# Three weight tiles ahead on ScalarE, one-hots of four tokens at once, and row fetches before bulk loads, in the gate stage of a two-layer kernel

## The reference

```python
vals, ci = lax.top_k(cand, P_TOPK)
e = (jnp.take_along_axis(i1, ci // P_TOPK, axis=-1) * N_KEYS
     + jnp.take_along_axis(i2, ci % P_TOPK, axis=-1))
g = jax.nn.softmax(vals, axis=-1)
...
a = jnp.einsum('cd,ckd->ck', xc, expert_u[ec])
w = (gc * jax.nn.gelu(a.astype(jnp.float32))).astype(x.dtype)
return jnp.einsum('ck,ckd->cd', w, expert_v[ec])
```

## Time and profile before

| what | value |
|---|---|
| median of 3 runs | 2543.64 us |
| profiled execution | 2543.99 us, its span 2542.3 us |
| busy share of the span | PE 94%, DVE 58%, ACT 44%, POOL 15% |
| chain that ended last | PE 77%, DVE 12%, ACT 8%, DMA 1%, issue 1% |
| GELU of the U jobs (L1397) | 128 x 491 ns |
| `whi` (L410) and `wlo` (L414) | 398 x 1056 ns and 398 x 1225 ns |
| copies to `stage` (L1478) | 96 x 1132 ns |
| HBM traffic | 407.12 MB read, 52.43 MB written |

### The profile page before, as it was taken

One profiled execution on the slowest core, in us unless ns is written; L12 is line 12 of the kernel. 1 busy time (PEld: TensorE's weight loads), 2 busy tenths in 40 slices (PEclk: granted clock), 3 DMA queues, 4 the chain that ended last, 5 costly groups with the idle time before them and its releaser, 6 DMA issues.

```text
span 2542.3 us, 39573 instructions
## 1 busy us (share of the span) xinstructions
PE 2397.2 (94%) x14819; PEld 2116.5 (83%) x14819; DVE 1463.5 (58%) x3355; ACT 1115.1 (44%) x1958; POOL 374.0 (15%) x338
## 2 busy tenths in 40 slices
PE   7999999999999888999999998888878999999999
PEld 4888788888785555779999998888877999999999
DVE  4444444333654485441899998777758773444443
ACT  4444343222442376343433448877853332332322
POOL 0000000000200000100001002222334313433330
PEclk9999999999998799998999999999998999999999
DMA  4223222322430000121556658887899988999992
GB/s 151 99 74 100 90 97 77 100 88 87 163 107 21 1 1 1 50 100 67 160 160 188 203 167 290 292 282 274 286 335 357 340 285 327 347 362 332 357 352 102
DMA packets 131823, 462.11 MB, mean 182 GB/s; under 512 B 13840, under 2 KB 32528, under 8 KB 129888
## 3 DMA queue, kind: packets, MB, share of 16 engines
q1 hardware_dynamic: 75744, 233.87, 26.9%
q0 software_dynamic: 51440, 196.90, 21.5%
q10 hardware_dynamic: 4496, 29.36, 3.0%
HBM read 407.12 MB, written 52.43 MB: 181 GB/s over the span
## 4 chain that ended last, share of the span: by engine, by line
PE 77%; DVE 12%; ACT 8%; DMA 1%; issue 1%; POOL 0%; ACTq 0%; SPq 0%; DVEq 0%; POOLq 0%
PE bank L427 13%; PE bank L428 13%; PE bank L429 13%; PE bank L1092 7%; PE bank L1093 7%; PE bank L1094 7%; DVE wlo L414 3%; PE bank L1105 2%; ACT stage L1478 2%; PE bank L442 2%; ACT hot L1464 1%; PE bank L1060 1%; PE bank L524 1%; ACT hot L1459 1%; ACT whi L410 1%; PE bank L707 1%
## 5 line engine op out<-in xcount | busy, mean ns | idle before, releaser
L414 DVE TENSOR_TENSOR wlo<-raw,whi 128x1024 fp32r<-128x1024 f32 x398 | 485.5, 1225 | 540.0 <-ACT whi L410 482.3
L427 PE MATMUL bank<-act_hi,whi 128*128 128x384 f32 (+1 forms) x1968 | 730.4, 371 | 31.9 <-DVE wlo L414 18.4
L428 PE MATMUL bank<-act_lo,whi 128*128 128x384 f32 (+1 forms) x1968 | 718.8, 365 | 0.0
L429 PE MATMUL bank<-act_hi,wlo 128*128 128x384 f32 (+1 forms) x1968 | 718.0, 365 | 0.0
L410 ACT ACTIVATE whi<-raw 128x1024 fp32r<-128x1024 f32 x398 | 418.3, 1056 | 288.2 <-PE bank L1094 175.2
L427 PEld LDWEIGHTS bank<-act_hi,whi 128*128 128x128 f32 x1968 | 375.8, 191 | 81.5 <-DVE wlo L414 21.0
L429 PEld LDWEIGHTS bank<-act_hi,wlo 128*128 128x128 f32 x1968 | 375.5, 191 | 38.1
L428 PEld LDWEIGHTS bank<-act_lo,whi 128*128 128x128 f32 x1968 | 376.0, 191 | 35.7 <-issue 0.5
L1092 PE MATMUL bank<-h_hi,whi 128*128 128x384 f32 x1024 | 350.2, 342 | 6.5 <-DVE h_lo L2196 6.5
L1093 PE MATMUL bank<-h_lo,whi 128*128 128x384 f32 x1024 | 348.0, 340 | 0.0
L1094 PE MATMUL bank<-h_hi,wlo 128*128 128x384 f32 x1024 | 345.8, 338 | 0.0
(11 more groups left out here) (354 smaller groups left out, 2765.5 us busy)
## 6 DMA issues: line engine op xcount, KB each, us to landing
raw<-tiles SPq DMA_DIRECT2D x398, 512.0 KB
acts_dram<-gelu SPq DMA_DIRECT2D x128, 192.0 KB
gates_dram<-stage ACTq DMA_DIRECT2D x12, 2048.0 KB
wg<-gates_dram POOLq DMA_DIRECT2D x16, 1536.0 KB
hf<-acts_dram POOLq DMA_DIRECT2D x16, 1536.0 KB
bias<-alibi POOLq DMA_DIRECT2D x16, 256.0 KB, 3.0
w1s<-cmp_w POOLq DMA_DIRECT2D x1, 4096.0 KB, 13.8
res<-x_t ACTq DMA_DIRECT2D x4, 512.0 KB, 10.0
```

The lines of the kernel that those rows point to most:

```text
L414: dve.tensor_tensor(wlo[:, j.slot, :], raw[:, j.slot, :], whi[:, j.slot, :].bitcast(F32), ALU.subtract).then_inc(lo_made, 1)
L427: pe.matmul(to, wh, x, start=(kc == 0), stop=False)
L428: pe.matmul(to, wh, xl, start=False, stop=False)
L429: last = pe.matmul(to, wl, x, start=False, stop=(kc == KC - 1))
```

## The change

- ScalarE prepares `whi` three jobs ahead (HI_AHEAD) in the gate stage, in the U jobs behind it and in the V jobs. One extra `make_hi` ahead of the first step fills the gap. VectorE's `make_lo` stays at two.
- VectorE makes the four first one-hots of a group in one instruction (a comparison of two broadcast operands, 128 x 512), behind the two weighted ones.
- The copy to `stage` walks the same 512 elements in another order: before it read the bank densely and wrote every 32nd element; now it reads every 128th element of the bank and writes runs of 4 neighbours.
- 2 dots in every step (96 in the stage, before 80), then 1 in each of 8 jobs (before 2), then 24 in the V jobs (before 32). With them the steps that follow the last dot (V_HEAD, V_WEIGHTS, QUADS) come one group earlier.
- GpSimd issues loads for group 0, two row fetches, the loads for group 1, six row fetches and the memset, in that order.

```diff
-DOTS_GATES = [2, 2, 1]
-DOTS_REST = 2
+HI_AHEAD = 3
+DOTS_GATES = 2
+DOTS_REST = 1
-V_HEAD = 4
+V_HEAD = 3
-QUADS = {40 + r * 78 // 31: r for r in range(32)}
+QUADS = {32 + r * 86 // 31: r for r in range(32)}
...
             load_gates(0)
-            load_gates(1)
             for m in range(RING):
                 pool.wait_ge(acts_stored[m], 16 * 5)
             load_acts(0)
+            for n in range(SEEN_GATES + ROWS, SEEN_GATES + ROWS + 2):
+                gather(n)
+            load_gates(1)
             load_acts(1)
+            for n in range(SEEN_GATES + ROWS + 2, SEEN_U + ROWS):
+                gather(n)
             pool.memset(spread[0][:, :], 0.0).then_inc(S("spread_zeroed"), 1)
-            for n in range(SEEN_GATES + ROWS, SEEN_U + ROWS):
-                gather(n)
...
+            make_hi(act, Job(J_U + U_GATES).ahead())
             for q in range(DT // 8):
-                u_job(U_GATES + q)
+                u_job(U_GATES + q, HI_AHEAD)
...
-                    act.activation(stage[:, buf, :, t:t + 4].rearrange("p j t -> p t j"),
-                                   bank[4 + gi % 4][:, :].rearrange("p (t j) -> p t j", t=4),
+                    act.activation(stage[:, buf, :, t:t + 4],
+                                   bank[4 + gi % 4][:, :].rearrange("p (t j) -> p j t", t=4),
...
-                    for x in range(4):
-                        t = 4 * gi + x
-                        ins = dve.tensor_scalar(hot[:, gi % 4 * 4 + x, 0, :], iota, selT[:, 0, t:t + 1], None, ALU.is_equal)
-                        if x < 2:
-                            dve.tensor_scalar(hot[:, gi % 4 * 4 + x, 1, :], iota, selT[:, 1, t:t + 1],
-                                              selT[:, 2, t:t + 1], ALU.is_equal, ALU.mult)
-                    ins.then_inc(S("hot_made"), 1)
-                for _ in range(DOTS_GATES[q % 3]):
+                    t, slot = 4 * gi, gi % 4 * 4
+                    for x in range(2):
+                        dve.tensor_scalar(hot[:, slot + x, 1, :], iota, selT[:, 1, t + x:t + x + 1],
+                                          selT[:, 2, t + x:t + x + 1], ALU.is_equal, ALU.mult)
+                    dve.tensor_tensor(hot[:, slot:slot + 4, 0, :], iota.unsqueeze(1).broadcast_to((P, 4, P)),
+                                      selT[:, 0, t:t + 4].unsqueeze(2).broadcast_to((P, 4, P)),
+                                      ALU.is_equal).then_inc(S("hot_made"), 1)
+                for _ in range(DOTS_GATES):
```

More of the change, by code:

```diff
@@ L64 @@
 ROWS = 8
-DOTS_GATES = [2, 2, 1]
-DOTS_REST = 2
+HI_AHEAD = 3
+DOTS_GATES = 2
+DOTS_REST = 1
 DOTS_V = 1
-V_HEAD = 4
+V_HEAD = 3
 V_WEIGHTS = GJ * V_HEAD + 1
-QUADS = {40 + r * 78 // 31: r for r in range(32)}
-SEEN_GATES = sum(DOTS_GATES) * 16
+QUADS = {32 + r * 86 // 31: r for r in range(32)}
+SEEN_GATES = DOTS_GATES * DT // 8
 SEEN_U = SEEN_GATES + DOTS_REST * (P - U_REST)
@@ L1398, in activation_of, with u_job @@
                                ACT.Gelu_apprx_tanh).then_inc(taken[j.slot], 1)
-            def u_job(n):
+            def u_job(n, ahead=AHEAD):
                 j = Job(J_U + n)
-                make_hi(act, j.ahead())
+                make_hi(act, j.ahead(ahead))
                 activation_of(j, n // RING)
@@ L1485, in _ @@
             for n in range(U_REST, P):
-                u_job(n)
+                u_job(n, HI_AHEAD)
             def weigh_hi(grp, m):
@@ L1502, in _ @@
                     jj = GJ * grp + dc
-                    if not (last and dc + AHEAD >= KC):
-                        make_hi(act, Job(J_V + jj).ahead())
+                    if not (last and dc + HI_AHEAD >= KC):
+                        make_hi(act, Job(J_V + jj).ahead(HI_AHEAD))
                     if not last and dc >= LATE:
```

## The result

The changed kernel takes 2456.99 us (median of 4 runs, 2455.63 to 2459.88), the kernel before, beside it, 2546.16 us (4 runs, 2543.43 to 2550.14). The ratio is 0.965, 95% interval 0.9631 to 0.9669. The profiled execution has a span of 2454.1 us, 88.2 less than before, where 66.3 were forecast.

What follows compares the result with a forecast made beforehand. A circle of waits between engines was taken to bound the gate stage, late loads and a row fetch the passage behind it. From 2543.99 us, 45.6 (stage) and 20.7 (passage) came off: 2477.7, forecast 2478, range 2462 to 2508.

Steps and rivals of the forecast that it cites:

- The circle of waits: Gate stage: VectorE, ScalarE and TensorE wait for each other, 14.05 us per two jobs; three ahead makes it 4.7 a job.
- Rival 3: Gate stage: the circle is not the cause, another wait holds 7.37 us a step; 2523 us, chance 0.06.
- What is late next: Gate stage once the circle is open: ScalarE's 6.2 us plus 0.2 gives a 6.4 us step, gain 45.6 us.
- near equals: Gate stage: 0.2 us a step added because two or three engines of nearly equal work do not meet exactly.
- the passage: Last one-hot product to first V product: 57.7 us falls to 37, gain 20.7, bounds 8 and 23.
- ScalarE's own work: Gate stage: 6.02 us busy a step plus 0.2 for issuing gate stores, so 6.2.
- the signs that I named: Profile signs of being right, among them `whi` waits under 10 us, clock 1.00, ScalarE fullest, V product about 37 us behind.
- The copy: ScalarE's copy to `stage`: kept at 1132 ns, bounds 600 (ScalarE at 5.14 us a step) and 1490 ns (6.92).
- low end: Lower edge of the range: a gate-stage step of 6.1 us (gain 59.7) and 22 us behind the stage, 2462 us.
- One-hots and dots: VectorE, gate stage: joint comparison saves 0.4 us a step, extra dots cost 0.38; it stays at 5.75.
- Rival 1: Gate stage: DMA takes over, 6.7 us a step, a late gate store leaves 12 us behind; 2501 us, chance 0.16.
- Rivals 2 and 4: ScalarE's copy: at 1490 ns, 2502 us, chance 0.12; or strided PSUM read slows the kernel, 2569 us at 2.2 us, 0.05.

Runs made afterwards that it cites:

- the last experiment: Changed kernel without the third product (act_hi times wlo) in the 48 gate-stage jobs, leaving out part of the computation: 2447.88 us, one run.
- The early load: Changed kernel with group 0's activations loaded once TensorE has used the last one-hots, not behind the last gate store: 2456.47 us, in a second series 2452.39.

## Why the prediction was wrong

**The circle of waits** was read rightly. Three ahead opens it, and alone it takes the step from 7.37 to 5.97 us, 65.9 us of the stage. Rival 3 is out.

**What is late next** is the step that failed. I put ScalarE at 6.2 us and added 0.2 for near equals: 6.4. The step is 5.95, TensorE's own work. The stage gave 66.5 us where the sum had 45.6; these 20.9 us are the miss (88.2 - 66.3 = 21.9 in all; the passage is 0.3 under its term, and 1.3 lie ahead of the stage and behind the passage). Of the 0.45 us a step, 0.2 are ScalarE's own work, 0.2 the term for near equals, and the last 0.05 the lag that ScalarE could afford even with its old copy. Of the signs that I named, two did not come for this reason: the fullest engine is TensorE and not ScalarE, and the last one-hot product starts 281.5 us behind the first and not some 300.

- *ScalarE's own work* with the old copy is 6.00 us, not 6.2. I divided its busy time in a stage full of gaps by the steps, and then added the store issue. An instruction with a gap behind it counts in full, while back to back the next one starts before it ends: in the old-copy run a GELU of 0.46 us at 1701.59 is followed by the next instruction at 1701.96, and ScalarE is busy 254.94 us in 260, 5.85 a step, where the earlier trace rows gave 6.02. From GELU to the next GELU without a wait it is 5.83 us. In the trace before, one such turn was already 5.95 us (1702.79 to 1708.74). The store issue adds 0.17 a step, near the 0.2 that I allowed.
- *The copy* fell to the lower end of its bounds. I took the old 1132 ns, since one stride was traded for another; it is 579. ScalarE's own work is then 224.06 us busy in 260, 5.13 a step. But this did not matter for the step: with the old copy it is 5.96. The copy is worth some 5 us, 4.8 of them in the passage, where a late ScalarE delays the last store.
- *The 0.2 us for near equals* had no row behind them, and no run shows them. In the changed kernel with the old copy ScalarE (6.00), TensorE (5.95), VectorE (249.78 us busy in 260, 5.73) and a full DMA ran at 5.96 us a step. That the four slots of each buffer let one engine lag behind the others is my explanation; no run varied their number.

The bound of the stage was there in the earlier trace rows. My low end used 6.1 us for it and 22 us behind it, so the range ended at 2462, before the floor of 5.95 was reached. With that floor and my own term for the passage the sum is 2544 - 66.7 - 20.7 = 2456.6.

**One-hots and dots.** The price was right (683 ns), and nearly the saving: where VectorE sets the pace, a step is 6.04 us with single one-hots and 5.67 with the joint comparison (the last experiment), 0.37 less where I had 0.4. Single one-hots cost 0.09 us a step here, since VectorE passes TensorE by that much; I had counted the edit as free under a ScalarE at 6.2. The two edits belong together: the shorter one-hots pay for the extra dots.

**DMA.** The 362 GB/s of the earlier trace rows were not a limit. The Trainium skill (DMA: Bandwidth & Descriptors, Specifications) has 358 GB/s for a core that shares its HBM; 381 over 285 us, and 402 in the last experiment, stand against taking that as the bound here, where one core runs the program. Rival 1 is out.

**The read of PSUM.** Rivals 2 and 4 are out: ScalarE reads 512 bytes apart at no more than the price of a dense copy (579 ns against 600 in the earlier trace rows). The Trainium skill (Advanced Engine Details and Errata, Memory Cachelines) says of SBUF that two accesses in a line are needed for the full rate, and runs of 2 bear it out nearly in full (633 ns against 579 in runs of 4). What it says of PSUM, beside a rule for matmuls, is that every two consecutive elements should be neighbours; breaking that costs this read nothing (579 ns, no two of them neighbours).

**The passage.** 37 forecast, 37.3 measured, though not by my dates. Group 0 landed 32.8 us behind the last product and not 25.6: the loads were issued at 14.8 (12.9 expected), and the activations took 16.9 us to land. The queueing ate the slack, and TensorE waited 3.8 us. My own dates added up to 34.0 + 1.5 = 35.5, and a remnant that I did not work out made them 37. The early load, where group 0 is not late, takes 35.3. So the dates of the U jobs and of the last GELU were right, that of group 0 was 7 us too early, and that 37 met 37.3 is partly luck. That the dots' dates and not the load order remove the wait for rows was the mechanism as written.

**Behind it**, nothing: 1 us.

## What to carry to other kernels

When waits form a circle over several engines, count over how many jobs it closes; one more job of lead on one engine can be worth more than a shorter instruction in it: 65.9 us of the stage here, where the shorter copy alone gave 31.3. For the pace after the circle is open, read an engine's own time from start to start of the same instruction where nothing waits, and not from busy time in a stretch with gaps, and let the range reach down to the floor of the fullest engine. Here, with rings of four slots, engines within 5% of each other cost nothing in the stage; the lag of the slowest came due at its end.

## What the hardware showed that was not expected

A ScalarE copy of 512 fp32 elements from PSUM to SBUF takes 579 ns when it reads 512 bytes apart and writes runs of 4, 633 ns with runs of 2, and 1132 ns when it reads densely and writes single elements 128 bytes apart.

The profiles fall into two groups by when the gate stage begins: near 1520 us (before, changed, old copy, old load order, three ahead alone) and 1524 to 1526 (the others), though the edits touch nothing ahead of it. Runs of one kernel fall into both groups: the second series of the early load has 2452.04, 2452.07 and 2452.39 us, and 2457.87 and 2458.23. The split comes up in the second layer's attention, where TensorE has gaps. Here are two stretches of the changed kernel's second profile and of the early activations' second, columns as in the earlier trace rows:

```profile
820.00:850.00 30.00, 30.00 (x100) 14.54 (x100) 12.41 (x20) 11.43 (x20) 0.00 (x0) 0.76 0.00 0
850.00:880.00 30.00, 24.12 (x91) 15.29 (x90) 11.83 (x48) 14.22 (x27) 0.00 (x0) 0.67 0.00 1
```

```profile
820.00:850.00 30.00, 30.00 (x87) 13.71 (x86) 10.73 (x18) 9.95 (x17) 0.00 (x0) 0.68 0.00 0
850.00:880.00 30.00, 24.73 (x76) 14.32 (x75) 9.24 (x36) 15.38 (x29) 0.00 (x0) 0.61 0.00 1
```

The granted clock is 0.76 and 0.67 in the one, 0.68 and 0.61 in the other. All 14 profiles go with one or the other: 0.76 to 0.80 and 0.66 to 0.68 in the six that begin near 1520 us, 0.66 to 0.69 and 0.61 in the eight others. What decides between them stays open. It moves a run by up to 6 us, more than the early load is worth, and so differences between experiments were read from the stage and the passage.
